# Which second-table sums of a PEER layer are gathered, and when: tile 0 early in place of tile 6 at the end

## The reference

```python
q = (xf @ w_q).reshape(T, 8, 256)
s1 = einsum('thd,nd->thn', q[..., :128], k1); s2 = einsum('thd,nd->thn', q[..., 128:], k2)
v1, i1 = top_k(s1, 16); v2, i2 = top_k(s2, 16)
sc, pidx = top_k(v1[..., :, None] + v2[..., None, :], 16)      # over the 256 pairs
expert = i1[pidx // 16] * 128 + i2[pidx % 16]                   # 8 x 16 = 128 experts a token
g = softmax(sc)
act = gelu(einsum('td,tkd->tk', x, u_tab[expert]))              # first table: dots
out = einsum('tk,tkd->td', g * act, v_tab[expert])              # second table: sums
```

## Time and profile before

| | us |
|---|---|
| median of 3 runs (lowest, highest) | 3631.14 (3626.45, 3634.81) |
| the profiled execution | 3630.36 |
| its span | 3628.6 |
| busy: TensorE, VectorE, ScalarE, GpSimd | 3114.2, 2786.7, 1362.1, 1927.0 |
| first block of V on TensorE | 1723.8 |
| last block of V done | about 3317 |

### The profile page before, as it was taken

The page is one execution under the profiler, slowest core; times in us unless marked ns, Lnnn a source line. Parts: engine busy times, 40 slices in busy tenths (PEclk is TensorE's granted clock), DMA queues, the critical chain, the costliest instruction groups (busy, mean ns, idle before and its releaser), DMA issues.

```text
span 3628.6 us, 56362 instructions
## 1 busy us (share of the span) xinstructions
PE 3114.2 (86%) x17498; PEld 2475.6 (68%) x17498; DVE 2786.7 (77%) x5946; ACT 1362.1 (38%) x3035; POOL 1927.0 (53%) x1504
## 2 busy tenths in 40 slices
PE   7999999999999988987999999999989999994000
PEld 4777676666666657776878888888878888884000
DVE  3333336988889887778889988999998887667898
ACT  4333311222323221487555555555555554000000
POOL 0000003555566764344667676677666766676676
PEclk9999999999999999999999999999999999997555
DMA  8444444778889899678999999999999999999998
GB/s 261 141 129 132 151 125 155 247 242 261 276 299 331 310 340 321 220 264 289 370 388 397 392 373 391 372 384 399 383 347 384 385 401 404 404 410 347 342 352 304
DMA packets 435382, 1127.21 MB, mean 311 GB/s; under 512 B 41888, under 2 KB 174368, under 8 KB 435232
## 3 DMA queue, kind: packets, MB, share of 16 engines
q0 software_dynamic: 204800, 745.10, 55.5%
q1 hardware_dynamic: 225664, 370.51, 28.9%
q10 hardware_dynamic: 4768, 9.96, 0.7%
HBM read 1098.81 MB, written 26.62 MB: 310 GB/s over the span
## 4 chain that ended last, share of the span: by engine, by line
PE 36%; DVE 18%; DMA 14%; issue 14%; POOL 4%; ACT 1%; DVEq 0%; SPq 0%; ACTq 0%; POOLq 0%
PE vacc L902 11%; DMA rows<-in_peer_u,eidx 10%; PE vacc L2329 9%; DVE rows L1742 7%; PE vacc L873 5%; PE scat L2263 4%; POOL rows L1536 4%; DVE oh1w L1821 2%; PE vacc L2243 2%; DMA rows<-in_peer_v,eidx 1%; DMA vbuf<-in_peer_v 1%; DVE htok L1752 1%; DVE eidx L1634 1%; DVE oh L1816 1%; DMA rows<-in_peer_v,dots 1%
## 5 line engine op out<-in xcount | busy, mean ns | idle before, releaser
L1536 POOL DMA_INDIRECT rows<-in_peer_u,eidx x1088 | 1396.5, 1284 | 839.8 <-DVE dots L1742 440.0
L1742 DVE CUSTOM_DVE_ANT_0 rows<-rows,htok 128x1024 f32<-128x1024 f32 x1088 | 1310.9, 1227 | 189.3 <-DMA rows<-in_peer_u,eidx 170.7
L2329 PE MATMUL vacc<-W,vbuf 128*128 (+1 forms) x6144 | 1424.6, 387 | 35.4 <-DMA vbuf<-in_peer_v 28.5
L2329 PEld LDWEIGHTS vacc<-W,vbuf 128*128 128x128 f32 x6144 | 1155.9, 192 | 186.0 <-issue 35.7
L2076 ACT ACTIVATE oh<-iota,e2s 128x128 bf16<-128x128 f32 x1536 | 486.7, 391 | 14.3 <-DVE wpart L1792 6.9
L1520 POOL TENSOR_TENSOR hot<-hot,ccid 128x864 f32<-128x864 bf16 x68 | 131.7, 1939 | 659.4 <-DVE hot L1727 570.2
L902 PE MATMUL vacc<-W 128*128 128x384 f32 x1280 | 432.7, 494 | 1.2 <-ACTq L775 1.2
L1752 DVE SCALAR_TENSOR_TENSOR htok<-rows,dots,htok 128x1024 f32<-128x1024 f32 x256 | 329.0, 1285 | 74.3 <-DMA rows<-in_peer_v,eidx 66.2
L1536 POOL DMA_INDIRECT rows<-in_peer_v,eidx x256 | 306.5, 1197 | 124.0 <-issue 77.5
L902 PEld LDWEIGHTS vacc<-W 128*128 128x128 f32 x1280 | 241.5, 192 | 167.0 <-issue 7.6
L2083 ACT ACTIVATE W<-scat 128x256 f32 (+1 forms) x320 | 122.9, 384 | 571.1 <-PE scat L2316 525.0
(11 more groups left out here) (330 smaller groups left out, 2922.0 us busy)
## 6 DMA issues: line engine op xcount, KB each, us to landing
vbuf<-in_peer_v SPq DMA_DIRECT2D x384, 512.0 KB
W<-in_w_in SPq DMA_DIRECT2D x80, 512.0 KB
W<-in_wq SPq DMA_DIRECT2D x64, 512.0 KB
vbuf<-in_w_ada SPq DMA_DIRECT2D x9, 2048.0 KB, 8.1
rows<-in_peer_u,eidx POOLq DMA_INDIRECT x1088
W<-in_w_in SPq DMA_DIRECT2D x16, 1024.0 KB
W<-in_w_ada SPq DMA_DIRECT2D x3, 2048.0 KB, 16.1
W<-in_w_out SPq DMA_DIRECT2D x12, 512.0 KB, 10.6
```

Of the source, the lines that this page charges most:

```text
L1536: g.indirect_dma_start(rows[:, s, :], None, table[:, :], bass.IndirectOffsetOnAxis(ap=picked, axis=0)).then_inc(landed[s], 16)
L1742: v.tensor_tensor_reduce(rows[:, s, :], rows[:, s, :], htok[:, home, :], 1.0, 0.0, ALU.mult, ALU.add, dots_of(t)[:, c:c + 1]).then_inc(use ...
L2329: mm = pe.matmul(vacc[:, k, :], vbuf[:, s, k * P:(k + 1) * P], W[:, e1, :].rearrange("p o t -> p (o t)"), start=(clear and s == 0 and k % ...
```

## The change

It exchanges the roles of tiles 0 and 6. Tile 0 is no longer in a dense group; its 128 sums are jobs 320 to 447, ahead of the sample tile's. Tile 6 goes into a dense group, and the groups become 1-2, 3-4 and 5-6. Tile 7 keeps its sums, jobs 1280 to 1407, which are now the last ones; there are 1408 jobs before and after.

With it go these moves:

- The plan. 24 jobs (12 before) ahead of the mixer's second half, 152 (148) in its first four heads and 224 (190) in its last four, one unit more ahead of it. Row "x" is new (8 jobs between two residuals), "r" and "s" get 36 jobs (none before). Between quarters -2 and -1 stand the new rows "t" (128 jobs, units 17 to 20) and "k" (8 jobs), since tile 2's dots must be done before group 0 can be built. Quarter -1 has 32 jobs and one unit (28 and three), quarter 0 has 88 jobs and three units (72 and one), quarters 1 to 8 have 64 jobs, quarter 9 has 48, and 80 jobs follow it (320 before).
- TensorE runs `cross(3)` without batches and quarter -1's batches by themselves after it. The sample tile's sum and tile 0's transposes stand between quarters 10 and 11; the rest of the finishing follows quarter 11.
- VectorE does all of the finishing after the last job.
- Tile 0's sums are stored to `sum0` once they are done and loaded again in the last group; the residuals of tiles 0 and 7 have a buffer of their own (`xe`, in a part of `W` that is no longer in use). The other residuals are loaded in two halves.
- `wo_first`: the first three heads' share of the output product waits for two loads of `w_out`, no longer for six. `mix_vector` has one more place for a step.

The diff, cut to its core:

```diff
@@ job_starts, stages @@
         if t == 1:
-            sum0[SAMPLE] = at
-            at += width(SAMPLE)
-    for t in (NT - 3, NT - 2):
-        sum0[t] = at
-        at += width(t)
-    return dot0, sum0, at
+            for early in (0, SAMPLE):
+                sum0[early] = at
+                at += width(early)
+    sum0[NT - 2] = at
+    return dot0, sum0, at + P
...
-TAIL = DOT0[NT - 2] + P // 2
-HALF_B, END_B = 160, 350
+YARD, HALF_B, END_B = 24, 176, 400
+LEAD, LATE = 8, 48
+TAIL = SUM0[NT - 2] + LATE
...
-    q = DOT0[2]
-    rows = [("p", 0, 0, 0, 4, 4), ("y", 0, 12, 4, 5, 12), ("m", 12, HALF_B, 5, H + NSU, SLOTS * H // 2),
-            ("n", HALF_B, END_B, 12, 12, SLOTS * H // 2), ("z", END_B, q, 12, 12, 2 * KC),
-            ("r", q, q, 12, 14, 16), ("s", q, q, 14, 15, 8)]
-    cuts = [q, q + 28, q + 56] + [q + P + 64 * i for i in range(10)]
-    units = [15, 17, 20, 21, 23, 25, 27, 29, 31, 33, 36, 36, 36]
+    q, e = DOT0[2], END_B
+    rows = [("p", 0, 0, 0, 4, 4), ("y", 0, YARD, 4, 6, 12), ("m", YARD, HALF_B, 6, H + NSU, SLOTS * H // 2 + 1),
+            ("n", HALF_B, e, 12, 12, SLOTS * H // 2), ("x", e, e + 8, 12, 12, 1), ("z", e + 8, e + 38, 12, 12, 2 * KC),
+            ("r", e + 38, e + 62, 12, 14, 16), ("s", e + 62, e + 74, 14, 15, 8),
+            (FIRST_Q, e + 74, q, 15, 17, QB), ("t", q, q + P, 17, 21, QB), ("k", q + P, q + P + 8, 21, 21, 2),
+            (-1, q + P + 8, q + P + 40, 21, 22, QB), (0, q + P + 40, q + 2 * P, 22, 25, QB)]
+    units = [25, 28, 29, 31, 33, 36, 36, 36, 36]
+    for i in range(1, LAST_Q):
+        rows.append((i, DOT0[4] + 64 * (i - 1), DOT0[4] + 64 * i, units[i - 1], units[i], QB))
+    rows.append((LAST_Q, SUM0[NT - 2], TAIL, 36, 36, QB))
@@ mixed_low, first step @@
-                pe.wait_ge(wo_in, 96 * g + 96)
+                pe.wait_ge(wo_first, 32 * g + 32)
@@ sync @@
                 sp.dma_start(S["sums"], acc[SAMPLE]).then_inc(sum_out, 16)
+                sp.dma_start(S["sum0"], acc[0]).then_inc(sum_out, 16)
                 for g in range(NDG):
-                    h_load(2 * g + 3)
+                    if g == 0:
+                        h_load(3)
+                        h_load(4)
+                    elif g == 1:
+                        h_load(6)
                     v_stream(g, 0, cut)
                     if g < NDG - 1:
-                        h_load(2 * g + 4)
+                        h_load(2 * g + 5)
                     else:
...
+                        sp.wait_ge(v_used, g * NKEY + VB + HK)
+                        sp.dma_start(first_sum, S["sum0"]).then_inc(sum_out, 16)
+                        for e, t in enumerate((0, NT - 2)):
+                            sp.dma_start(xe[:, :, e * P:(e + 1) * P], S["x2"][:, :, column(t):column(t) + P].rearrange("k p t -> p k t")).then_inc(sum_out, 16)
@@ vector, after the residuals @@
+                for at in steps(plan["r"]):
+                    mixed_step(at)
+                scale(2)
+                for at in steps(plan["s"]):
+                    mixed_step(at)
+                quarter(plan[FIRST_Q])
                 summed_rows(SAMPLE)
+                for at in steps(plan["t"]):
+                    mixed_step(at)
+                behind = steps(plan["k"])
+                mixed_step(next(behind))
+                soft_high(1)
                 picks_low(1)
...
+                mixed_step(next(behind))
+                picks_high(1)
+                for i in range(-1, LAST_Q + 1):
@@ vector, after the last job @@
                 summed_rows(NT - 2)
+                sample_sums()
+                tile_finish(0)
+                finish(NDG - 1)
+                sample_norm()
+                tile_norm(0)
                 tile_finish(1)
+                norm(NDG - 1)
                 tile_norm(1)
@@ tensor @@
                 cross(2, scattered)
-                cross(3, lambda x: scattered(16 + x))
+                cross(3, lambda x: None)
                 pe.wait_ge(s_ready, NUNIT)
                 pe.wait_ge(tr_free, NT)
+                turn(1)
+                for b in range(QB, 2 * QB):
+                    batch(b, b, first_scat)
...
                     if not last:
                         turn(2 * g + 3)
+                    else:
+                        pe.wait_ge(sum_out, 96)
+                        pe.wait_ge(acc_ready, 2)
...
+                        tile_turn(0)
                     quarter(4 * g + 3, not last)
```

## The result

The changed kernel takes 3723.6 us (3715.7 to 3728.1) where the kernel before took 3630.6 on the same chip: a ratio of 1.0254 (95% interval 1.0233 to 1.0275), 2.5% slower, 93 us. The forecast was 3626 us, with a range of 3578 to 3682. Its profiled execution took 3728.1 us, with a span of 3726.3, 97.7 more than before's.

A forecast was written before the change was run, and what follows sets the result against it. It took VectorE as busy and DMA as full from 1720 us on, with a 312 us tail after TensorE stops; terms A to G summed to -5 us, giving a 3626 us median, range 3578 to 3682.

The forecast's parts named there:

- C: Quarter -2: the two units and the batches stay, ten more jobs come as sums at 1.32 us each, +13 us.
- E: Quarter -1: 32 jobs and one unit instead of 28 and three, ScalarE now binds with it at 90 us, -18 us.
- A: The mixer, heads 0 to 7 (618 to 1369 us): more jobs, partly covered by VectorE's idle time, +17 us.
- absorbed: Faster rival: the mixer's 34 added jobs fit into VectorE's idle time; total 3580 us, chance 0.23 (below 3603).
- B: Residuals to quarter -2 (1369 to 1513 us): loses tile 1's picks, gains 36 sums, +32 us (28 to 36).
- D: New stretches "t" and "k" ahead of quarter -1: 208 us (200 to 235) and 20 us, together +228 us.
- F: Quarters 0 to 9: the same 648 jobs lying otherwise, 14 units instead of 16, +24 us (0 to +45).
- G: From the end of the plan to the end: 269 us after against 570 before, -301 us.
- Six buffers: Slower rival: six gather buffers limit heads 4 to 7 (106 us a head) and t (225); total 3690 us, chance 0.18.
- Bandwidth: Slower rival: V and gathers together never pass 360 GB/s, 1619 us against 1603 in F and G; 3642 us, chance 0.03.
- The stop between quarters 10 and 11: Sums' loads and a mask ahead of quarter 11's blocks; job 1352 done well before TensorE comes, price small.
- The cold array: TensorE pauses some 150 us before quarter 0 and would start at 1.2 GHz; a few us at most.

The follow-up runs named there:

- plain loads: Changed kernel where jobs 176 to 399 and 512 to 639 load 128 consecutive table rows by plain instead of indirect load: heads 97, 96, 101, 104 us, t 215.9 us.
- the mend: Changed kernel with unit 14's score reload ahead of gather 456 instead of 447, and the last loads spread between V's blocks: 3690.7 us, ratio 1.0181.
- thin vector work: Changed kernel where VectorE takes 256 of 1024 columns in jobs 176 to 399 and 512 to 639, gathers whole: heads 95, 88, 93, 93 us, t 207 us.
- the five buffers: Changed kernel with five gather buffers in rotation instead of six, the sixth's memory still reserved: 3789.6 us.

## Why the prediction was wrong

The reading of what bounds the kernel was right in direction: VectorE ahead of the first dense quarter takes back what the tail gives. The sizes on that side failed, all one way but in C, which held, and E.

**A (+17, was +57).** The step that failed is "I take +5, +11, +4 and +5 for heads 4 to 7". It let VectorE's idle time of 9 to 16 us a head take a third to a half of the new work. The heads took +11, +18, +15 and +11. VectorE's busy time rose by 11, 11, 14 and 11 us, 47 of the 56, and its idle time did not fall: 60 us in the four heads, before 50. That idle time is of two kinds. Waiting for gathers is 43 us of the 60 after, 32 of the 50 before, and 14 of 32 with plain loads; the rest, part of it waiting for ScalarE, is 17 to 19 us in all three. So the second kind took in nothing, and the first kind grew, because GpSimd issues late. The dots' share of the waits, before and after (the sums' stand in the rows further down):

```profile
DVE rows L1742 <- DMA rows<-in_peer_u,eidx: 26.2, 28, 2.1
```
```profile
DVE rows L1763 <- DMA rows<-in_peer_u,eidx: 33.6, 35, 2.9
```

GpSimd's price stood in no term of A, though its issue fills the second head nearly whole: 77.1 us busy and 17.3 between gathers, 94 of 105 us.

```profile
L1557 POOL DMA_INDIRECT rows<-in_peer_u,eidx x57 | 77.1, 1352 | 29.4 <-issue 17.3 <-DVE dots L1763 12.2
```

With plain loads the heads are 27 us longer than before's, close to the 25 forecast; the kernel before was never run with plain loads, so this is no proof that the forecast's cover exists. A second error is in the price of the work. The 34 jobs more were taken at 1.16 us each, 10 us a head. But tile 0's sums begin at job 320, so the four heads lose 16 dots and gain 50 sums, and these take longer: 46 us more of VectorE by their two lines, where 40 stood. The sums of the four heads together, before and after:

```profile
L1752 DVE SCALAR_TENSOR_TENSOR htok<-rows,rss,htok 128x1024 f32<-128x1024 f32 x26 | 33.4, 1285 | 6.3 <-DMA rows<-in_peer_v,dots 5.6 <-DVE W L1199 0.2
```
```profile
L1773 DVE SCALAR_TENSOR_TENSOR vbuf<-rows,dots,vbuf 128x1024 f32<-128x1024 f32 x76 | 97.7, 1285 | 13.1 <-DMA rows<-in_peer_v,eidx 9.3 <-DVE W L1205 0.8 <-issue 0.6
```

The kernel before shows the slope of 1.54 us a job as well, at 47 jobs a head and for sums; the evidence that I had cited against "absorbed" (81 us busy in a head of 96) should have set the sum. The terms ahead of these heads held: head 4 starts at 993 us in both traces. The -6 for the split wait can't be told from nothing.

**B (+32, was +51).** The sums had their size. Missing is the queue on GpSimd that I did not walk through: moving the units against the gathers put a reload behind a store that had just begun, 16 us by the mend. The prediction walked through SyncE's queue (in D) and not through GpSimd's.

**C (+13)** held to half a microsecond: chained sums at 1.32.

**D (+228, was +260).** "k" held. In t the step "200 us of VectorE, some gathers late, 208" priced a job by VectorE alone. GpSimd's price, 1.28 us and 0.30 to the next, was in the trace of the kernel before, on its page:

```profile
L1536 POOL DMA_INDIRECT rows<-in_peer_u,eidx x1088 | 1396.5, 1284 | 839.8 <-DVE dots L1742 440.0
```

The earlier trace rows has GpSimd busy 84 to 95 us in each quarter of 64 jobs, and it was never in the sum: 128 x 1.59 + 13.3 for the units' products is 217 us, more than VectorE's 197. Two engines that full, coupled by six buffers, took 239. The coupling shows in t's rows: GpSimd waits 28 us for VectorE to free a buffer (its row above), and VectorE waits 36 us for gathers:

```profile
DVE rows L1763 <- DMA rows<-in_peer_u,eidx: 36.0, 48, 2.4
```

The plain loads took 23 us of it away.

**E (-18, was -36).** ScalarE's 85 us were carried over; in the changed kernel it has 68 in this quarter, and 72 is its length. TensorE, at a granted clock of 0.50, is busy 25 us of it.

**F (+24, was +43).** Quarters 0 to 9 came at 174, 141, 131, 136, 130, 147, 135, 145, 121, 123 against 179, 144, 126, 136, 131, 145, 131, 127, 121, 124. Nearly all of the miss is quarter 7. The prediction priced the store and load there at nothing. In the kernel before three units on VectorE cover them: its quarter 7 took 146 us with both, and the changed kernel's quarter 5 took 147 with three units and neither. Taking that cover away uncovered 16 to 20 us. The price could have been read before: quarter 11, without units, has the same store and load, took 133 us, and TensorE waits in it twice for a block of V, once after each:

```profile
PE vacc L2329 <- DMA vbuf<-in_peer_v: 15.1, 2, 7.9
```

**G (-301, was -289).** End steps 22.6 us against 24, quarter 11 111 us. Quarter 10 took 142 where 124 stood: the step "5 for 2.25 MB of loads" priced their bytes, where SyncE's issue of them and of the next block took 24 us. Spreading them gave 16 back.

**The rivals.** "Six buffers" gave 106 us a head, and the heads took 105 to 110, which is luck: its mechanism is not the cause there, as the thin vector work (56 gathers in 88 us) and the five buffers show, and its total of 3690 was also passed. It does describe the tail. "Absorbed" is refuted. "Bandwidth": quarter 8 ran at 393 GB/s and the last sums at 398, and t with plain loads reached 368 where 333 were seen, so bandwidth did not set it. The stop between quarters 10 and 11 cost nothing at its own place; its loads cost quarter 10 the 16 us above. The cold array cost 2 us: TensorE's first block, after a stretch at a granted clock of 0.50, took 5.82 us, the next 3.69. The prediction's "no stretch from 1719 on is below 360" leaves out the tail, at 341. The page's 358 GB/s (the Trainium skill, DMA: Bandwidth & Descriptors, Specifications) is again below what the core moved, 398 GB/s over 155 us.

The range was too narrow because its upper end was one rival's cost, while four terms (A, B, D, F) each left out a cost and so were wrong the same way. The heads and F came near the upper ends of their own ranges (+60 and +45), and B and t passed theirs (+36 and 235); the total's range was not built from these.

## What to carry to other kernels

Before moving work to where an engine looks idle, ask what the idle time waits for: if it lies inside a chain through that engine, or waits for another engine that is itself nearly full, work put into it adds its whole length and more (here 1.5 to 1.8 us a job of 1.3). Price a moved step on every engine that issues it, GpSimd and SyncE too, and walk each of their queues in order for what now stands in front of it. And look first for a cheap cure at the place that is slow: buffers idle in the tail gave 19 us, moving the tail's work cost 93.

## What the runs showed of the hardware

- GpSimd's time for the same indirect gather depends on what VectorE does beside it. In t it is 1.29 us with full dots, 1.35 with full dots and a quarter of the bytes, and 0.96 with quarter dots and full bytes. A plain load of the same size takes it 0.53.
- Six gathers in flight can carry one job per 1.57 us with DMA full (share 1.02, 380 GB/s, the second head with thin vector work).
- SyncE was held 1.5 to 11.2 us by each of four loads in a row, issued while gathers and V filled the DMA engines (quarter 10), against 0.33 for V's own block issued just before. With the loads of x2 in halves and apart, each took it 0.38. That a queue with no room left holds it is my reading.
